# Router logits by token, counting split in two, selection ahead of the weights, and a tile-by-tile final norm

## The reference

```
h = rms_norm(x, norm_moe)
g_logits = h @ w_group + b_group                   # 4 groups, softmax, argmax
e_logits = h @ w_router + b_router                 # 8 experts in each group
within = e_logits of the chosen group; top 2; weight = g_prob * softmax(top 2)
for each of 32 experts e, over the tokens that chose it:
    y = (silu(h @ w1[e]) * (h @ w3[e])) @ w2[e]    # 1024 -> 512 -> 1024
x = x + sum of weight * y
out = rms_norm(x, final_norm)
```

## Time and profile before

| what | value |
|---|---|
| median of three runs | 707.66 us (706.98 to 707.76) |
| the profiled execution: its own time | 707.0 us |
| its span, first to last instruction | 705.2 us |
| PE busy | 515.7 us (73%) |
| PE weight loads | 326.1 us (46%) |
| DVE busy | 201.5 us (29%) |
| ACT busy | 145.1 us (21%) |
| POOL busy | 16.5 us (2%) |
| DMA queue of SP | 243.62 MB, 85.7% of 16 engines' span |
| HBM read | 242.53 MB |
| mean granted TensorE clock | 0.885 |

### The profile page before, as it was taken

The page is one execution under the profiler, slowest core; times in us unless marked ns, Lnnn a source line. Parts: engine busy times, 40 slices in busy tenths (PEclk is TensorE's granted clock), DMA queues, the critical chain, the costliest instruction groups (busy, mean ns, idle before and its releaser), DMA issues.

```text
span 705.2 us, 8763 instructions
## 1 busy us (share of the span) xinstructions
PE 515.7 (73%) x3815; PEld 326.1 (46%) x3815; DVE 201.5 (29%) x368; ACT 145.1 (21%) x250; POOL 16.5 (2%) x28
## 2 busy tenths in 40 slices
PE   6999899999999888855945673473584557347483
PEld 5899799898998663321411131141141114114121
DVE  3697645478765440100100000010010001001002
ACT  6564445354434441000000000000000000000002
POOL 1200000001001000000000000000000000000001
PEclk9999999999999999887887797796788779779688
DMA  9899233606499898999999999999999999999991
GB/s 294 240 352 374 102 120 120 239 1 214 151 353 355 338 398 325 429 427 428 426 429 428 426 427 427 431 427 427 426 428 429 429 427 427 427 427 429 419 394 79
DMA packets 48089, 244.21 MB, mean 346 GB/s; under 512 B 8936, under 2 KB 18352, under 8 KB 37296
## 3 DMA queue, kind: packets, MB, share of 16 engines
q1 hardware_dynamic: 48048, 243.62, 85.7%
HBM read 242.53 MB, written 4.22 MB: 350 GB/s over the span
## 4 chain that ended last, share of the span: by engine, by line
PE 49%; DMA 43%; ACT 3%; DVE 3%; issue 2%; SPq 1%; POOL 0%; POOLq 0%; PEldq 0%; DVEq 0%; ACTq 0%
PE ps L640 15%; DMA slots_own<-in_w 12%; DMA slots_late<-in_w 12%; PE ps L933 10%; DMA attn_data<-in_w 8%; PE ps L659 7%; PE ps L938 6%; DMA slot_mixed<-in_w 4%; DMA slot_spare<-in_w 4%; PE ps L618 1%; PE ps L947 1%; DMA slots_own<-in_w_in 1%; PE ps L1005 1%; PE ps L685 1%; SPq L505 1%
## 5 line engine op out<-in xcount | busy, mean ns | idle before, releaser
L933 PE MATMUL ps<-slots_late,x_sb 128*32 128x512 f32 x336 | 88.9, 686 | 38.7 <-DMA slot_mixed<-in_w 16.1
L933 PE MATMUL ps<-attn_data,x_sb 128*32 128x512 f32 x176 | 72.0, 708 | 21.7 <-DMA slots_own<-in_w 21.7
L1584 DVE TENSOR_TENSOR bqT<-ps,bqT 128x512 f32<-128x512 f32 x8 | 5.5, 692 | 236.2 <-ACT bqT L1248 236.2
L938 PE MATMUL ps<-slots_own,vb 128*32 128x512 f32 x192 | 54.7, 727 | 23.8 <-DMA slot_spare<-in_w 8.8
L410 DVE TENSOR_TENSOR w_low<-slots_own,w_high 128x2048 fp32r<-128x2048 f32 (+1 forms) x32 | 64.7, 2022 | 24.2 <-ACT w_high L1061 24.0
L1245 ACT ACTIVATE vb<-ps 128x256 f32<-128x256 f32 x8 | 3.1, 384 | 309.6 <-PE ps L975 309.6
L933 PE MATMUL ps<-slot_spare,x_sb 128*32 128x512 f32 x112 | 51.4, 664 | 14.5 <-DMA attn_data<-in_w 14.5
L933 PE MATMUL ps<-slots_own,x_sb 128*32 128x512 f32 x240 | 55.2, 665 | 5.9 <-DMA slot_spare<-in_w 3.2
L1061 ACT ACTIVATE w_high<-slots_own 128x2048 fp32r<-128x2048 f32 (+1 forms) x32 | 54.2, 1694 | 21.6 <-PE ps L659 10.8
L640 PE MATMUL ps<-h_high,w_high 128*128 128x256 f32 x224 | 56.3, 291 | 0.0
L933 PEld LDWEIGHTS ps<-slots_late,x_sb 128*32 128x32 f32 x336 | 22.6, 124 | 71.7 <-issue 71.7
(11 more groups left out here) (263 smaller groups left out, 929.9 us busy)
## 6 DMA issues: line engine op xcount, KB each, us to landing
slots_own<-in_w SPq DMA_DIRECT2D x27, 2048.0 KB, 34.2
slots_late<-in_w SPq DMA_DIRECT2D x26, 2048.0 KB, 34.9
attn_data<-in_w SPq DMA_DIRECT2D x17, 2048.0 KB, 34.5
slot_last<-in_w SPq DMA_DIRECT2D x9, 2048.0 KB, 36.4
slot_spare<-in_w SPq DMA_DIRECT2D x9, 2048.0 KB, 34.1
slots_own<-in_w_in SPq DMA_DIRECT2D x8, 2048.0 KB, 11.7
slot_mixed<-in_w SPq DMA_DIRECT2D x8, 2048.0 KB, 32.6
slots_own<-in_w_out SPq DMA_DIRECT2D x2, 2048.0 KB, 7.8
```

What stands on the lines that cost most here:

```text
L933: return pe.matmul(ps[SLOTS * e:SLOTS * e + SLOTS, 4 + matrix, :], xeT[:, k, SLOTS * e:SLOTS * e + SLOTS], w, start=(k == 0), stop=(k == K ...
L938: return pe.matmul(ps[SLOTS * e:SLOTS * e + SLOTS, 4 + c, :], actT[:, f, SLOTS * e:SLOTS * e + SLOTS], w, start=(f == 0), stop=(f == FC - ...
L1584: dve.tensor_tensor(act_sb, ps[:, 5, :].rearrange("p (q f) -> p f q", f=FC), silu_sb.rearrange("p (f q) -> p f q", f=FC), ALU.mult).then_i ...
```

## The change

- `route(t)` swaps the operands: tokens stand in the array, the 36 weight columns stream. The logits come out by token, 128 x 36, where DVE reads them; the two ACT copies and the two turns are gone. `logits_done` is raised by `route`.
- The rank products raise `rank_done` after three; the two count products go to another bank and raise `count_done`.
- DVE makes `place` right behind `rank_done`, then `sel` of step 0; the largest count and the weights of the choice (`finish_routing`) come between `sel` and `selw` of step 0. PE waits for `count_read` at the fifth of eight column blocks of the first gather.
- The residual sums start in four pieces: three ahead of the rank products, one behind the counts.
- The last additions go tile by tile (`top_done`, `added`). ACT squares each tile behind its own signal; the small product now stands inside the `If`. DVE does gain and root of each tile in one instruction for each 512 columns, and SP writes four pieces.

```diff
@@ SP
             for t in range(TT):
-                sp.wait_ge(out_set[t], 1)
-                sp.dma_start(out_v[:, t, :], xn[:, t, :]).then_inc(out_written, 16)
-            sp.wait_ge(out_written, 16 * TT)
+                for c in range(2):
+                    sp.wait_ge(out_set[t], c + 1)
+                    sp.dma_start(out_v[:, t, 512 * c:512 * c + 512], xn[:, t, 512 * c:512 * c + 512]).then_inc(out_written, 16)
+            sp.wait_ge(out_written, 16 * 2 * TT)
@@ PE
-                    m = pe.matmul(ps[0:N_RT, 6 + t, 0:P], w_rt[:, k, :], xT[:, k, t * P:(t + 1) * P],
+                    m = pe.matmul(ps[:, 6 + t, P:P + N_RT], xT[:, k, t * P:(t + 1) * P], w_rt[:, k, :],
                                   start=(k == 0), stop=(k == KD - 1))
-                m.then_inc(logitsT_done, 1)
+                m.then_inc(logits_done, 1)
-            for t in range(TT):
-                pe.wait_ge(logitsT_copied, t + 1)
-                m = pe.transpose(ps[:, 6 + t, P:P + N_RT], rlT[:, t * P:(t + 1) * P], ident[0:N_RT, 0:N_RT])
-                m.then_inc(logits_done, 1)
-            start_sum(0)
+            start_sum(0, 0)
+            start_sum(0, 1)
+            start_sum(1, 0)
             pe.wait_ge(routed, 1)
-            pe.matmul(ps[:, 6, EXPERTS:2 * EXPERTS], one, chosen[:, 0, :], start=False, stop=True)
-            pe.matmul(ps[:, 6, 2 * EXPERTS:3 * EXPERTS], one, chosen[:, 0, :], start=True, stop=False)
-            pe.matmul(ps[:, 6, 2 * EXPERTS:3 * EXPERTS], one, chosen[:, 1, :], start=False,
-                      stop=True).then_inc(count_done, 1)
-            start_sum(1)
-            pe.wait_ge(count_read, 1)
+            pe.matmul(ps[:, 6, EXPERTS:2 * EXPERTS], one, chosen[:, 0, :], start=False, stop=True).then_inc(rank_done, 1)
+            pe.matmul(ps[:, 7, 0:EXPERTS], one, chosen[:, 0, :], start=True, stop=False)
+            pe.matmul(ps[:, 7, 0:EXPERTS], one, chosen[:, 1, :], start=False, stop=True).then_inc(count_done, 1)
+            start_sum(1, 1)
                 for k in range(KD):
+                    if slices_in and k == 4:
+                        pe.wait_ge(count_read, 1)
-                for c in range(2):
-                    pe.wait_ge((y_copied_a, y_copied_v)[c], it + 2)
-                    for t in range(TT):
+                for t in range(TT):
+                    for c in range(2):
+                        pe.wait_ge((y_copied_a, y_copied_v)[c], it + 2)
                         m = pe.matmul(ps[:, 2 * t + c, :], ...)
+                    if t == 0 and slices_out:
+                        m.then_inc(top_done, 1)
                 m.then_inc(added, 1)
@@ ACT
-            act.wait_ge(logitsT_done, 1)
-            act.activation(rlT[:, 0:P], ps[0:N_RT, 6, 0:P], ACT.Copy).then_inc(logitsT_copied, 1)
-            act.wait_ge(logitsT_done, 2)
-            act.activation(rlT[:, P:T], ps[0:N_RT, 7, 0:P], ACT.Copy).then_inc(logitsT_copied, 1)
-            act.wait_ge(moe_done, 1)
-            square(ps[:, 0:2, :], 5, 0, x_sb[:, 0, :]..., fsq)
-            act.wait_ge(gained, 1)
-            square(ps[:, 2:4, :], 5, 1, x_sb[:, 1, :]..., fsq)
-            act.wait_ge(frstd_set, 2)
-            act.activation(xn[:, 1, :], xn[:, 1, :], ACT.Copy, scale=rstd[:, 5, 1:2]).then_inc(out_set[1], 1)
+            for t in range(TT):
+                act.wait_ge((top_done, added)[t], (1, STEPS + 1)[t])
+                square(ps[:, 2 * t:2 * t + 2, :], 5, t, xn[:, t, :].rearrange("p (a b) -> p a b", a=2), fsq)
@@ DVE
-            dve.wait_ge(rexp_set, 1)
-            ... the weights of the choice ...
-            dve.wait_ge(count_done, 1)
+            dve.wait_ge(rank_done, 1)
             dve.scalar_tensor_tensor(place, ...).then_inc(moved, 1)
+            def finish_routing():
+                dve.wait_ge(count_done, 1)
+                dve.tensor_reduce(most[:], ps[:, 7, 0:EXPERTS], AX_X, ALU.max).then_inc(count_read, 1)
+                dve.wait_ge(rexp_set, 1)
+                ... the weights of the choice ...
+                dve.wait_ge(count_read, 1)
+                dve.tensor_copy(most_i[:], most[:]).then_inc(most_set, 1)
                 dve.tensor_tensor(sel, ...).then_inc(sel_made, 1)
+                if first:
+                    finish_routing()
                 dve.wait_ge(sel_made, it + 1)
                 dve.tensor_tensor(selw, sel, ...)
-            dve.wait_ge(moe_done, 1)
-            for t in (1, 0):
-                if t == 0:
-                    dve.wait_ge(fsq, 1)
-                dve.tensor_tensor(xn[:, t, :]..., ps[:, 2 * t:2 * t + 2, :], fgain..., ALU.mult).then_inc(gained, 1)
-            dve.wait_ge(gained, 2)
-            dve.wait_ge(frstd_set, 1)
-            dve.tensor_scalar(xn[:, 0, :], xn[:, 0, :], rstd[:, 5, 0:1], None, ALU.mult).then_inc(out_set[0], 1)
+            for t in range(TT):
+                dve.wait_ge(frstd_set, t + 1)
+                for c in range(2):
+                    dve.scalar_tensor_tensor(xn[:, t, 512 * c:512 * c + 512], ps[:, 2 * t + c, :], rstd[:, 5, t:t + 1],
+                                             fgain[:, 512 * c:512 * c + 512], ALU.mult, ALU.mult).then_inc(out_set[t], 1)
```

More of the change, by code:

```diff
@@ L258, in decoder_layer @@
         xT = ga
-        rlT = probT[0:N_RT, 0, 0, 0:T]
         xeT = x_sb[:, 0, :].rearrange("p (k s) -> p k s", k=KD)
@@ L314, in decoder_layer @@
         router_set, xturned, xT_copied = sem("router_set"), sem("xturned"), sem("xT_copied")
-        logitsT_done, logitsT_copied, logits_done, count_done, count_read, qscale_set = (
-            sem("logitsT_done"), sem("logitsT_copied"), sem("logits_done"), sem("count_done"), sem("count_read"),
-            sem("qscale_set"))
+        logits_done, rank_done, count_done, count_read, qscale_set = (
+            sem("logits_done"), sem("rank_done"), sem("count_done"), sem("count_read"), sem("qscale_set"))
         rexp_asked, rexp_set = sem("rexp_asked"), sem("rexp_set")
@@ L325, in decoder_layer @@
             sem("y_left_done"), sem("y_copied_a"), sem("y_copied_v"), sem("added"))
-        moe_done, fsq, frstd_set, gained, out_written = (
-            sem("moe_done"), sem("fsq"), sem("frstd_set"), sem("gained"), sem("out_written"))
+        top_done, again_done, fsq, frstd_set, out_written = (
+            sem("top_done"), sem("again_done"), sem("fsq"), sem("frstd_set"), sem("out_written"))
         out_set = [sem(f"out_set{t}") for t in range(TT)]
@@ L899, in _, with start_sum @@
             route(1)
-            for t in range(TT):
-                pe.wait_ge(logitsT_copied, t + 1)
-                m = pe.transpose(ps[:, 6 + t, P:P + N_RT], rlT[:, t * P:(t + 1) * P], ident[0:N_RT, 0:N_RT])
-                m.then_inc(logits_done, 1)
             job_evacuated(pe, "xo3")
             job_evacuated(pe, "xo2")
-            def start_sum(t):
-                for c in range(2):
-                    pe.matmul(ps[:, 2 * t + c, :], ident, x_sb[:, t, 512 * c:512 * c + 512],
-                              start=True, stop=True, skip_group_check=True)
-            start_sum(0)
+            def start_sum(t, c):
+                pe.matmul(ps[:, 2 * t + c, :], ident, x_sb[:, t, 512 * c:512 * c + 512],
+                          start=True, stop=True, skip_group_check=True)
+            start_sum(0, 0)
+            start_sum(0, 1)
+            start_sum(1, 0)
             pe.wait_ge(const_in, 16)
@@ L1032, in _ @@
                                 expert_step((g + r * TURNS) * UNROLL + u, unit_again)
-            pe.matmul(ps[0:1, 6, 0:1], ident[:, 0:1], ident[:, 0:1], start=True, stop=True).then_inc(moe_done, 1)
+                pe.matmul(ps[0:1, 6, 0:1], ident[:, 0:1], ident[:, 0:1], start=True, stop=True).then_inc(again_done, 1)
         @block.scalar
@@ L1264, in _ @@
                                 expert_step((g + r * TURNS) * UNROLL + u)
-            act.wait_ge(moe_done, 1)
-            square(ps[:, 0:2, :], 5, 0, x_sb[:, 0, :].rearrange("p (a b) -> p a b", a=2), fsq)
-            act.wait_ge(gained, 1)
-            square(ps[:, 2:4, :], 5, 1, x_sb[:, 1, :].rearrange("p (a b) -> p a b", a=2), fsq)
-            act.wait_ge(frstd_set, 2)
-            act.activation(xn[:, 1, :], xn[:, 1, :], ACT.Copy, scale=rstd[:, 5, 1:2]).then_inc(out_set[1], 1)
+                act.wait_ge(again_done, 1)
+            for t in range(TT):
+                act.wait_ge((top_done, added)[t], (1, STEPS + 1)[t])
+                square(ps[:, 2 * t:2 * t + 2, :], 5, t, xn[:, t, :].rearrange("p (a b) -> p a b", a=2), fsq)
         @block.vector
@@ L1545, in _ @@
                               ALU.subtract).then_inc(rexp_asked, 1)
-            dve.wait_ge(rexp_set, 1)
+            weight = rt[:, 11]
+            place = rt[:, 9]
             dve.wait_ge(routed, 1)
[L1549 to L1552, removed]
@@ L1553, in _ @@
-            then(dve.reciprocal(rs[:, 3, :], rs[:, 2, :]))
-            weight = rt[:, 11]
```

(24 more changed lines are left out.)

3 lines of the change are left out of this document (1 added, 2 removed).

## The result

Median of 13 runs: 704.25 us (701.52 to 706.08), against 707.55 us (705.07 to 711.06) for 13 runs of the kernel before. The ratio is 0.9936, 95% interval 0.9918 to 0.9954: 4.5 us faster, between 3.3 and 5.8. I had forecast 702.0 from 707.66, 5.65 us.

What follows compares the result with a forecast made beforehand. The weight stream was taken as the bound, leaving only its start and the tail behind its last byte. Head 2.5 plus tail 3.15 gave 5.65 us, from 707.66 to 702.0 us; range 700.8 to 704.4.

Steps and rivals of the forecast that it cites:

- What bounds the kernel: Expert steps: the weight stream runs without a gap from the twelfth load, so its end is that instant plus a constant.
- Rival A: Expert steps: the stream does not take over the head's gain, only the tail counts; 704.5 us, chance 0.10.
- a flow that would be over before the restart: Before the twelfth load: old loads end by 266 whatever the change does, leaving about 1 us of gap.
- Steps 1 to 3: Routing head: logits 0.95 us earlier, sel at 258.35, gather at 259.45 instead of 261.95; gain 2.5 us, bounds 1.9 to 2.8.
- the 0.27: Routing logits: estimated us per swapped product if loads do not overlap, making the head gain 0.2 us less; not adopted.
- Step 4: Routing behind sel: largest count, weights and selw end at 260.8, hidden with 0.6 us left; cost nothing.
- Steps 5 to 9: Tail: additions and norm by tile save 2.8 us, smaller last write 0.35; together 3.15, bounds 2.3 to 3.4.
- Rival B: Tail: it gives little because ACT's or DVE's fetch behind the branch is late; 704.0 us, chance 0.08.
- the last additions start at 689.8: Tail, expected sign: last additions start at 689.8 us instead of 692.26.
- tile 1 at 695.94 as now: Last additions: tile 0 complete at 694.1, tile 1 at an unchanged 695.94, from four products of 0.92 us.
- rival D: Gather and step 0: PE's clock falls to its lower level, the stream starves; 712.5 us, slower, chance 0.03.

Runs made afterwards that it cites:

- e12: The changed kernel executed once more, unchanged, for a profile; 7.22 us from the last slice's first product to the end of the last addition, no ratio given.
- e4: Changed kernel plus ten identity products on PE in front of the last weight slice, result unused; 0.9910 of the kernel before, median 702.17 us.
- e2: Kernel before with only the tail of the change (additions and final norm by token tile), routing as before; 706.95 us, ratio 0.9977.
- e8: Changed kernel plus twelve identity products between sel and step 0's gather; twelfth load 2.68 us later behind the cross-attention's last sum, no ratio given.
- e1: Kernel before with only the routing part of the change, additions and final norm as before; 704.59 us, ratio 0.9946.
- e11: Kernel before with the routing part but without logits by token; twelfth load 15.88 us after the cross-attention's last sum (before 17.67), no ratio given.
- e7: Kernel before with the logits by token alone; twelfth load 15.97 us after the cross-attention's last sum (before 17.67), no ratio given.
- e6: Changed kernel with the ten identity products and the fourth residual-sum piece moved behind step 0's w1 and w3 products; ratio 0.9915.

## Why the prediction was right, and where its sum was off

**What bounds the kernel** held to a tenth of a microsecond: from the twelfth load to the last slice's first product it is 422.5 to 422.7 us in all eleven profiles without added products there, whether the load went 2.8 us earlier or 2.7 later. Rival A, a stream that does not take the gain over, is out. One premise of mine was wrong and did no harm: I counted on a flow that would be over before the restart, with about 1 us of the gap left. The last old load (the gain's, issued at 257.85, 10.7 us to landing) landed at 268.6, behind the restart at 268.00, and still nothing of the gain was lost. An edit that moves the restart further forward can no longer count on a gap.

**Steps 1 to 3, the head, 2.5 us**: measured 2.77. The logits gained 0.98 (I had 0.95), sel came at the place for which I had 258.35 (258.58 with x taken off), the gather at 259.30 (259.45). PE's signals (260.4 to 260.9) did not wait for the array. A swapped product went at 1.93 / 8 = 0.24 us in the busy time and 0.22 in the chain; no sign of the 0.27 that I had worked out from what the Trainium skill ("TensorE: Matmul & The Clock Gate", "The mechanism") says of loads that do not overlap, and the measurement decides. What I had not seen is that the swap alone also shortens DVE's wait for the exponentials and so brings 1.70; beside the new order that part is worth nothing more.

**Step 4**, what was moved behind sel: hidden, with 0.54 us left (I had 0.6).

**Steps 5 to 9, the tail, 3.15 us**: d fell from 9.28, 8.95 and 8.99 to 5.99, 5.99 and 6.22, means 9.07 and 6.07, so 3.0. POOL took 0.19 us both times, the second time (699.03) beside DVE's new instructions for tile 0 (698.24 to 699.65), so these do not hold it up. The Trainium skill ("SBUF — State Buffer", "SBUF: two separate sides") has DVE lock POOL out in a two-port mode or with two SBUF inputs; the trace agrees, if the root, read as a scalar, does not count as a second input. The writes of a quarter MB landed in 2.0 to 2.3 us instead of 2.6 (I had taken 0.35 off), in e12 in 2.3 to 2.7. Rival B is out: ACT squared tile 0 at 2.4 us into the additions, not waiting for its branch.

**The term that was missing** is in c. The step of the prediction that failed is the one that took the last slice's products and the additions at their old lengths ("the last additions start at 689.8", "tile 1 at 695.94 as now"): the clock falls about when the last slice is begun, the products take 3.18 instead of 1.92, the additions 4.04 instead of 3.63, and c grows by 1.67 us (7.22 against 5.55 on average). I had the low clock as rival D, but at the gather and as a disaster; it came at the other end and took more than a quarter of the gain. With it the sum is 2.77 + 3.0 - 1.67 = 4.1 us, inside the measured 3.3 to 5.8. That the low clock costs this much is shown by e4, where c returns to 5.52. That the median of 704.25 lies in my range, which ends at 704.4, is in part luck: it is nearer to rival A's 704.5 than to my 702.0, and only the traces tell the two apart.

**Why the new routing meets the low clock** is not settled. In the changed kernel PE waits longer for the last slice (2.48, 2.40 and 2.44 us in its three profiles; 1.68, 1.79 and 1.64 before), because PE had worked through the last step's first products faster. The windows of the last step show it, before and after:

```profile
674.00:676.00 2.00, 2.00 (x16) 0.59 (x12) 0.00 (x0) 0.00 (x0) 0.00 (x0) 0.63 1.02 408
```

```profile
674.00:676.00 2.00, 2.00 (x23) 0.54 (x16) 0.00 (x0) 0.00 (x0) 0.00 (x0) 0.99 1.03 410
```

PE had resumed at 670.17 and 670.39, at the low level in both, and rose sooner in the changed kernel. That explains the longer wait, but not yet the clock behind it. In the eleven profiles without products added in front of the last slice, the clock stayed up behind the four shorter waits (1.64, 1.68, 1.79 and, in e2, 2.00 us) and fell with the seven longer ones (2.17 in e8, 2.31 in e1, 2.40 to 2.48 in the changed kernel, 2.91 in e11, 2.92 in e7); in e4, which fills the wait, it stayed up. The two nearest, e2 and e8 (PE's timeline; the wait is in the brackets):

```profile
690.27 1.92 PE L939 MATMUL ps<-slots_late,vb 128*32 128x512 f32 x16 [2.00 <-DMA slots_late<-in_w]
```

```profile
692.75 2.54 PE L931 MATMUL ps<-slots_late,vb 128*32 128x512 f32 x16 [2.17 <-DMA slots_late<-in_w]
```

So the wait is the likely cause, but no run changed its length alone. The instant at which the stream restarts is not what decides: in e8 it is where it was before (a 17.58 against 17.67), and the clock fell all the same.

**The scatter at the front** is open too. x lay between 249.4 and 250.4 in the five profiles with the old routing and between 248.3 and 253.3 in the nine others, though nothing ahead of x was changed; where it was over 251, a low clock shows between 150 and 200 us (0.97 on average there, 1.00 elsewhere). Nine against five is too few to say that the change does it. It could explain why the two medians (3.3 us apart) differ less than the parts; this is not shown.

**The better version** by its c and its median is e4: 0.9910 of the kernel before, 0.9878 to 0.9941, beside 0.9934 (0.9909 to 0.9960) for the changed kernel on the same chip.

## What to carry to other kernels

Where a saturated stream sets the end, find the one instant from which it runs without a gap. Here an edit ahead of it moved the end by what it moved the instant, forwards (e1) and backwards (e8), to 0.1 us. That an edit inside the stream is worth nothing was argued from the same reading and not tested by itself. When two edits shorten the same wait, they do not add; ask of each what it does to every operand of the waiting instruction. And a sum that keeps the length of the last stage "as now" should name the clock it was measured at: where PE waits ahead of the last stage, a few products of no use in the gap can be worth something: here 1.7 us, beside 2.8 and 3.0 for the two reorderings.

## What the runs showed of the hardware

- The weight stream repeats to 0.12 us either way in 422.6 (85 loads of 2 MB), over eleven executions of seven programs.
- PE granted at half clock costs on this path 1.5 to 1.7 us out of 5.6, and ten products of 0.24 us in the wait ahead of it kept the clock up in both profiles of the changed kernel that had them (e4 and e6).
- A change 420 us earlier goes with a clock that falls in the last 6 us: in all seven profiles with a part of the new routing, in none of the four without it. The moved restart of the stream does not account for it (e8), and the cause is open.
